# Latent attention heads on one core: the next head's query transposes and splits in front of the attention output

## What is computed

```python
def _expand_latent(c, w_ukv, g_knope):
    kv = jnp.einsum('bsc,chd->bshd', c, w_ukv)
    kn = _rms_norm(kv[..., :QK_NOPE_DIM], g_knope)
    return kn, kv[..., QK_NOPE_DIM:]

def _mla_block(qn, qr, qpos, kn, kr, v, kpos):
    logits = (jnp.einsum('bqhd,bkhd->bhqk', qn, kn, preferred_element_type=jnp.float32)
              + jnp.einsum('bqhr,bkr->bhqk', qr, kr, preferred_element_type=jnp.float32)) * MLA_SCALE
    mask = (kpos // CHUNK)[None, :] <= (qpos // CHUNK)[:, None]
    p = jax.nn.softmax(jnp.where(mask, logits, NEG_INF), axis=-1)
    return jnp.einsum('bhqk,bkhd->bqhd', p.astype(v.dtype), v)
```

## Time and profile before

| | |
|---|---|
| median of 3 runs | 2337.19 us (2335.77 to 2338.96) |
| profiled execution, its own time | 2336.79 us |
| its span in the profile | 2335.0 us |
| PE busy | 2228.4 us, 95% |
| DVE busy | 1135.4 us, 49% |
| ACT busy | 914.8 us, 39% |
| `block_f` (first to last matmul) | 1686 to 2116 us |
| PE, DVE, ACT busy in it | 410.5, 313.6, 212.4 us |
| from T0 to T0, middle heads | 25.9 us |

### The profile page before, as it was taken

The page is one execution under the profiler, slowest core; times in us unless marked ns, Lnnn a source line. Parts: engine busy times, 40 slices in busy tenths (PEclk is TensorE's granted clock), DMA queues, the critical chain, the costliest instruction groups (busy, mean ns, idle before and its releaser), DMA issues. The chain is left out here.

```text
span 2335.0 us, 33484 instructions
## 1 busy us (share of the span) xinstructions
PE 2228.4 (95%) x11777; PEld 1899.0 (81%) x11777; DVE 1135.4 (49%) x2619; ACT 914.8 (39%) x1953; POOL 219.3 (9%) x234
## 2 busy tenths in 40 slices
PE   8999999999999999999998999989699999998998
PEld 6888888888888888778878878868688999886887
DVE  5554444544454444452332433325577777774222
ACT  5444444444444444432232332324345455543111
POOL 0100000000000000000000000005721111100000
PEclk9999999999999999999999999999999999998999
DMA  4323333333333323224324223333321111103331
GB/s 170 107 97 105 100 100 105 104 97 105 98 103 98 96 97 105 96 74 156 123 85 124 96 72 102 102 99 102 130 71 59 45 53 45 59 28 131 127 126 68
DMA packets 106111, 225.21 MB, mean 96 GB/s; under 512 B 10385, under 2 KB 45457, under 8 KB 105921
## 3 DMA queue, kind: packets, MB, share of 16 engines
q1 hardware_dynamic: 106048, 224.35, 29.9%
HBM read 191.42 MB, written 32.89 MB: 96 GB/s over the span
## 5 line engine op out<-in xcount | busy, mean ns | idle before, releaser
L216 PE MATMUL bank<-b_whi,x_hi 128*128 128x512 f32 x1024 | 405.1, 396 | 10.7 <-DVE b_wlo L199 10.7
L216 PE MATMUL bank<-b_whi,x_lo 128*128 128x512 f32 x1024 | 400.6, 391 | 0.0
L216 PE MATMUL bank<-b_wlo,x_hi 128*128 128x512 f32 x1024 | 400.4, 391 | 0.0
L199 DVE SCALAR_TENSOR_TENSOR b_wlo<-b_raw,g_fox,b_whi 128x512 fp32r<-128x512 f32 x256 | 180.9, 748 | 146.4 <-ACT b_whi L186 145.9
L186 ACT ACTIVATE b_whi<-b_raw,g_fox 128x512 fp32r<-128x512 f32 x256 | 170.6, 715 | 164.2 <-PE bank L216 142.4
L216 PEld LDWEIGHTS bank<-b_whi,x_hi 128*128 128x128 f32 x1024 | 192.8, 188 | 47.7 <-DVE b_wlo L199 10.9
L216 PEld LDWEIGHTS bank<-b_whi,x_lo 128*128 128x128 f32 x1024 | 192.6, 188 | 41.5
L216 PEld LDWEIGHTS bank<-b_wlo,x_hi 128*128 128x128 f32 x1024 | 192.8, 188 | 36.0
L216 PE MATMUL bank<-m_whi,x_hi 128*128 128x512 f32 x320 | 125.6, 393 | 0.8 <-DVE m_wlo L199 0.8
L216 PE MATMUL bank<-m_wlo,x_hi 128*128 128x512 f32 x320 | 125.2, 391 | 0.0
L216 PE MATMUL bank<-m_whi,x_lo 128*128 128x512 f32 x320 | 125.0, 391 | 0.0
(11 more groups left out here) (467 smaller groups left out, 5008.2 us busy)
## 6 DMA issues: line engine op xcount, KB each, us to landing
b_raw<-w_fox SPq DMA_DIRECT2D x128, 512.0 KB, 3.5
m_raw<-w_mla SPq DMA_DIRECT2D x40, 512.0 KB, 3.4
c_raw<-w_out SPq DMA_DIRECT2D x32, 512.0 KB, 3.5
g_raw<-w_out SPq DMA_DIRECT2D x32, 512.0 KB, 3.6
f_raw<-w_ukv SPq DMA_DIRECT2D x16, 512.0 KB, 3.5
queries<-e_q SPq DMA_DIRECT2D x16, 480.0 KB, 3.3
f_q<-queries SPq DMA_DIRECT2D x16, 480.0 KB, 3.3
e_raw<-w_uq SPq DMA_DIRECT2D x16, 384.0 KB, 3.4
```

Of the source, the lines that this page charges most:

```text
L199: op = eng.scalar_tensor_tensor(lo[:, k, :], raw[:, k, :], self.gain[:, K:K + 1], hi32[:, k, :], ALU.mult, ALU.subtract)
L216: op = eng.matmul(out, a, w[:, k, :], start=(first and k == 0 and i == 0), stop=(last and k == self.kk - 1 and i == len(pairs) - 1))
```

## The change

`qn` and `qr` leave the head of the list and stand now, for the head that comes next, between `ont` and `o`. They are tied to the tiles' head h (whose keys are just finished) by the list `NEXT`; in the bodies they run as jobs of `h - 1` in a count that is one head ahead (`ahead`). With the list the bank of every job shifts: `qn` takes bank 7, `qr` bank 5, `o` keeps bank 6, `kp` goes from 6 to 5, and `ont` from 5 to 6. The second half of the keys and the values that follow it stand now behind `kp`. The single weight slot and the single value buffer stay, and so do the value splits behind `o`.

```diff
-    ORDER = ["qn", "kp", "qr", "T0", "T1", "s3", "ka", "T2", "s2", "new", "T3", "s1", "s0", "T8", "sa", "sb", "T4",
-             "p3", "T5", "pn", "p2", "p1", "T6", "on", "p0", "g", "T7", "ont", "o"]
+    ORDER = ["kp", "T0", "T1", "s3", "ka", "T2", "s2", "new", "T3", "s1", "s0", "T8", "sa", "sb", "T4",
+             "p3", "T5", "pn", "p2", "p1", "T6", "on", "p0", "g", "T7", "ont", "qn", "qr", "o"]
+    NEXT = ("qn", "qr")
...
-    SPLITS = ["qn", "kp", "qr", "ka", "new", "p3", "pn", "p2", "p1", "p0"]
+    SPLITS = ["kp", "ka", "new", "p3", "pn", "p2", "p1", "p0", "qn", "qr"]
...
-        for b, k in map(self.job, self.FROM.get(name, ())):
+        for n in self.FROM.get(name, ()):
+            b, k = self.job(n)
+            if n in self.NEXT:
+                k -= self.use[b]
...
-                self.q_in.wait(eng, g, 1)
+                self.q_in.wait(eng, g + 1, 1)
...
             def body(h, last, g):
                 for name in H.ORDER:
-                    if name[0] != "T":
+                    if name in H.NEXT:
+                        if h is not None:
+                            H.dve_job(dve, h - 1, name, o_all)
+                    elif name[0] != "T":
...
-                    if g is not None and name == "qr":
+                    if g is not None and name == "kp":
                         H.dve_keys(dve, g, 1)
                         for b in (2, 3, 4):
                             H.dve_values(dve, g, b)
```

More of the change, by code:

```diff
@@ L60, with __init__ @@
 class Sig:
-    def __init__(self, sem, per=1, unit=1, credit=0):
-        self.sem, self.per, self.unit, self.credit = sem, per, unit, credit
+    def __init__(self, sem, per=1, unit=1, credit=0, ahead=0):
+        self.sem, self.per, self.unit, self.credit, self.ahead = sem, per, unit, credit, ahead
     def grant(self, eng):
@@ L70, in wait @@
     def wait(self, eng, step, k):
-        v = (step * self.per + k + self.credit) * self.unit
+        v = (step * self.per + k + self.credit + self.ahead) * self.unit
         if not isinstance(v, int) or v > 0:
@@ L125, in packer, with sem @@
         return place
-    def sem(self, name, per=1, unit=1, credit=0):
+    def sem(self, name, per=1, unit=1, credit=0, ahead=0):
         handle = self.nc.alloc_semaphore(name)
         self.used.append(handle)
-        return Sig(handle, per, unit, credit)
+        return Sig(handle, per, unit, credit, ahead)
     def clear_old(self, eng, keep):
@@ L1950, in __init__ @@
         self.use = [sum(1 for i in range(len(self.JOBS)) if i % 3 == b) for b in range(3)]
-        self.ready = [s(f"f_ready{b}", n) for b, n in enumerate(self.use)]
-        self.free = [s(f"f_free{b}", n, credit=1) for b, n in enumerate(self.use)]
+        turned = [sum(1 for n in self.NEXT if self.job(n)[0] == b) for b in range(3)]
+        assert all(self.job(n)[1] == self.use[self.job(n)[0]] for n in self.NEXT)
+        self.ready = [s(f"f_ready{b}", n, ahead=turned[b]) for b, n in enumerate(self.use)]
+        self.free = [s(f"f_free{b}", n, credit=1, ahead=turned[b]) for b, n in enumerate(self.use)]
         self.kv_done = self.G.done
@@ L1960, in __init__ @@
         self.v_lo = s("f_v_lo", TT)
-        self.hi_done = s("f_hi_done", len(self.SPLITS))
+        self.hi_done = s("f_hi_done", len(self.SPLITS), ahead=len(self.NEXT))
         self.new_max, self.negmax = s("f_new_max", 2), s("f_negmax", TT)
@@ L2328, in body @@
                 for name in H.ORDER:
-                    if name[0] != "T":
+                    if name in H.NEXT:
+                        if h is not None:
+                            H.act_job(act_, h - 1, name, o_all)
+                    elif name[0] != "T":
                         if g is not None:
@@ L2406, in body @@
                 for name in H.ORDER:
-                    if name[0] != "T":
+                    if name in H.NEXT:
+                        if h is not None:
+                            H.pe_job(pe, h - 1, name)
+                    elif name[0] != "T":
                         if g is not None:
```

## The result

The changed kernel takes 2346.1 us (median of 6 runs, 2345.1 to 2348.6) against 2337.7 for the kernel before (6 runs): 0.38% slower, ratio 1.0038 with a 95% interval of 1.0026 to 1.0049. 2343.1 was predicted, with a range of 2338.8 to 2347.5. The profiled execution has a span of 2343.8 us, 8.8 more than before.

What follows compares the result with a forecast made beforehand. PE, busy 95%, was taken to wait for DVE at each head turn. 14 turns +5.3, first turn +1.4, last turn -0.4 make +6.3 us on 2336.79: 2343.1 us, range 2338.8 to 2347.5.

Steps and rivals of the forecast that it cites:

- What bounds the turn: Between `ont` and T0, PE is short of DVE; DVE's own queue is the longer of two nearly equal chains.
- Step 1: PE from `ont` to `o`: `o` waits for ACT's copy of `ont` and starts 1.3 us later than before.
- Step 2: DVE's row after the low weights: `qnlo`, `qr`'s split, `o_mla`, one `f_v`, from 1832.21 to 1834.68 us.
- Step 3: Start of T0 in each turn: it waits for the first `f_v`, +0.36 us, taken as +0.38 per turn.
- Step 4: Rest of the head after T0: second half of the keys starts at 1835.7 against 1835.99; nothing new is late.
- Step 5: Sum over the turns: 14 x 0.38 = +5.3, first turn +1.4 for two splits, last turn -0.4; together +6.3 us.
- a rival for every turn: PE stops three times per turn and its clock falls to 0.68: 2.0 us more, 15 times, 2373 us; chance 0.03.
- The last turn: Turn without new weights or T0: `o` 1.23 later, then `o_mla`, `f_v` twice and `kplo`; -0.4 us in all.
- the second rival: DVE's queue closes up at each turn, all starts overlapping and hand-offs shortest: no change, 2339.8 us; chance 0.30.

Runs made afterwards that it cites:

- half of the move: Against the changed kernel, only `qn` moves in front of `o` while `qr` stays behind `kp`; 2340.4 us, ratio 1.0013 to the kernel before.

## Why the prediction was right, and where it was off

**What bounds the turn: right.** PE was short of DVE, and the change put 1.4 us more in front of the value that T0 waits for. That T0 waits for `f_v`, two experiments show, each with `o` unmoved: values ahead of `o_mla` (-0.37 per turn) and a second value buffer (-0.56). The prediction also called DVE's queue "the longer of two nearly equal chains", and that is how it is: by 0.05 us. Two weight slots, which take 1.23 us out of the queue, give back only 0.08.

**Step 1, PE up to `o`: right in size, by luck, since the reason was wrong.** 1.60 measured, 1.67 predicted. I had ACT's copy of `ont` hold `o`. PE's own `qn` (0.58) and `qr` (0.66) took until the same moment, and without the copy's delay `o` was no earlier.

**Step 2, DVE's row: right.** Predicted from the low weights' end: `qnlo` -0.08, `qr` +0.03, `o_mla` +0.04, `f_v` -0.08. Measured: -0.09, +0.04, +0.03, -0.09. The rule on quadrants of partitions that the Trainium skill gives (VectorE: DVE Perf Modes, "Two Vector instructions with no wait between them") fits this trace too; in half of the move, where `o_mla` follows `qnlo` and no quadrant changes, it starts 0.07 before `qnlo` ends:

```profile
1911.77 0.68 DVE L2194 TENSOR_TENSOR f_qnlo<-bank,f_qnhi 128x512 fp32r<-128x512 f32 x1
1912.38 0.68 DVE L2213 TENSOR_TENSOR o_mla<-bank,f_gt 128x512 f32 x1
```

**Step 3, T0: right.** +0.33 measured, +0.36 worked out; I took +0.38. In sum 5.0 us (from `s3` to the last-but-one `ont`) against 5.3. The waits divide otherwise than foretold: 0.32 ahead of T0 instead of 0.6, and 0.39 ahead of `kp`, which was to be the shorter one.

**Step 4, the rest of the head: right.** No new wait is seen there in the waits of PE.

**Step 5, the first turn: half of it missing.** +1.4 was predicted, +2.96 measured, counted from the first `f_k`. The half that the step worked out was right: `f_v` came 1.43 later, as its sum has it, and T0 1.47. That `kp` now waits for `qr`'s split it overlooked, but beside `f_v` this cost next to nothing. What it had at nothing was the clock ("PE's busy time and its clock stay"): it fell behind the wait of 2.9 to 4.0 us and cost some 1.5. I had written the falling clock down as a rival for every turn and spoke against it with the first turn of the kernel before. It does not fall at the 14 turns, where the waits are 0.39 and 0.32; it falls at the first.

**The last turn: right.** -0.35 measured, -0.4 predicted.

Together the parts make 5.0 + 2.96 - 0.35 = 7.6 us; 8.4 were measured between the medians, with an interval from 6.1 to 11.5. The rest of about 0.8 us is not placed.

That 2346.1 lies within the range is in part luck. The upper end, 2347.5, was made from turns of +0.55, which did not come; the clock, which was in no term, took up that room. The forecast also stands on the 2336.79 of the profiled execution, the second rival and the range on the median of 2337.19: on the median it would have been 2343.5.

## What to carry to other kernels

When work is moved to cover an engine's wait, follow it on the engine that is waited for, and count what now stands between the last thing it did and the value that ends the wait; here PE got cover, DVE's queue got 1.4 us longer, and `o`, which the same value also stands behind, came 1.24 us later. Moving work and freeing the buffers that force the order behind it were each worth nothing or less, and together 0.3%. And look at the turns that a loop makes only once: with one wait of 3 to 4 us, the first turn cost as much as nine of the regular ones, half of it by the clock.

## What the runs showed of the hardware

Between the end of PE's last matmul of `o` and DVE's `o_mla`, where DVE had been idle, it was 0.24 us in the loop (1912.66 to 1912.90) and 0.04 outside it (2090.96 to 2091.00 in the earlier trace rows). The loops with both buffers double show 0.23 to 0.25 as well, with the move and without it. In the loop the values that DVE's waits compare with come from registers (the `REGISTER_ALU` in the orders above); that this makes the difference was not tried. T0's own wait for `f_v` cost 0.05 to 0.06, at the first turn as in the loop.

In the second profile of the changed kernel, after a wait of 4.0 us, PE was still at the upper level when it began again at 1706.74 (matmuls of 256 columns 0.12 us apart at 1707.34), and at 1707.86 it was at the lower one (0.22 apart). In the first profile of the changed kernel, after 2.9 us, the transposes of `kp` were slow already (0.92 us against 0.65), and in half of the move, after 4.4 us, all the more (1.11). The price falls on what PE does behind the wait, here `kp`, T0 and T1, and comes to some 1.5 us; the row that shows the wait does not show it.
